# Bit search of a top-k threshold written out in three groups of blocks, with the mixer's operations placed singly among the bits

## The chip, the cores and the metric

The kernel runs on one core of a Trainium2 chip. The metric is the device time of one execution, in microseconds (us). The kernel is written with its own semaphores and its own order of instructions on every engine: TensorE (PE), VectorE (DVE), ScalarE (ACT), GpSimd (POOL) and SyncE (SP).

## The reference, cut to what matters

The whole is a two-layer decoder trunk over 1024 positions of width 1024. The change touches one stage of layer 0. There, every query position picks the 256 keys with the largest indexer scores, and mixer A, a short gated convolution, is computed beside it:

```python
isc = jnp.where(causal[None], isc, -jnp.inf)      # scores, Q_BLOCK = 128 queries at a time
_, idx = lax.top_k(isc, topk)                     # topk = 256
...
bg, cg, hv = jnp.split(sc, 3, axis=-1)            # 3 x 512 columns of h @ w_in
ya = bg * causal_dwconv(cg * hv, conv_w)          # CONV_WIDTH = 3
```

Only the threshold, the 256th largest score of each query, has to be found before the attention can mask its keys.

## The kernel before

**Blocks.** Queries are cut into 8 blocks of 128; block b has a score tile of 128 partitions (one query each) by 128(b+1) keys. Blocks 0 and 1 have at most 256 keys and need no search. The six others are searched together: DVE counts blocks 5, 4 and 3 (768, 640 and 512 columns), ACT counts blocks 7, 6 and 2 (1024, 896 and 384 columns).

**Search.** The threshold is built bit by bit, 31 times after the sign. Each round needs, for every block, the number of scores that reach a candidate. DVE's `count` is a `tensor_scalar` that compares and accumulates; ACT's is a `Sign` activation that accumulates. Then six candidates, one column each of the tile `srch` (128 partitions by 11 rows by 8), are updated together: `S_TRY` is the candidate with the next bit flipped (L1965, two tensors), the counts are compared with a row of limits (L1971, two tensors), the outcome is compared with the sign (L1972, two tensors), and L1974 (a `scalar_tensor_tensor`) shifts it into place and writes the new candidates. Both engines run a loop over bits. ACT counts all three of its blocks, and only then is `act_counted` raised; DVE writes all six candidates at once, and `cand_ready` lets both engines into the next bit.

**Mixer A.** PE computes 12 weight units (`ev_sc`, four tiles of three) of 48 matmuls each (`three_pass`, L859) into pairs of PSUM banks. POOL splits each unit's weights into a high and a low part beforehand: `w_scaled` (L592), `w_hi` (L593), `w_lo` (L595); the split of unit n+2 waits until PE has finished unit n. Tile i of the mixer is computed after bits 8i to 8i+7 (the last after seven bits) by `mixer_a(i)` on both engines, in one piece: ACT copies the first unit out (L1437), DVE multiplies it by the second (L2023), ACT makes the first tap (L1439), DVE adds the other two taps (L2028, twice) and multiplies by the third unit (L2033), ACT makes the high half (L1442) and DVE the low half (L2036). PE's next unit of a kind waits for the copy of the last one of that kind (`a_cg`, `a_prod`, `a_f`).

**After it.** PE waits for the last `a_f` and then computes the first attention scores (L1223); DVE masks them (L2066), in a stage written out by hand (`attend`), into which the end of the search (`resolve`) is placed. `ev_out`, the feed-forward layers and layer 1 follow.

The setup of the search is `search_begin`: it adds the causal mask to each tile, counts once against zero for the sign and writes the first candidates (L1946).

Of the kernel before, what the change touches and what calls it, by code (L numbers as in the profile page):

```python
# [27 lines left out]
P = 128  # L28
# [39 lines left out]
BY_DVE = [5, 4, 3]  # L68
BY_ACT = [7, 6, 2]
SEARCH = BY_DVE + BY_ACT  # L70
SIGN_BIT = -2 ** 31
# [16 lines left out]
def build(nc, t, out, stop=None):  # L88
    ctx = ExitStack()
    with ctx:  # L90
# [98 lines left out]
        (S_V, S_CAND, S_COUNT, S_NEG, S_TAKE, S_NEGI, S_BIT, S_NEAR, S_TRY, S_BACK, S_LIM) = range(11)  # L189
# [591 lines left out]
        def _(pe):  # L781
# [420 lines left out]
            with pe.Fori(0, 2) as i:  # L1202
                for ti in range(2):
                    tile = i * 2 + ti
                    for g in range(3):
                        unit = unit0["ev_sc"] + i * 6 + 3 * ti + g
                        pe.wait_ge((a_cg, a_prod, a_f)[g], tile + 1)
                        pe.wait_ge(w_split, unit + 1)
                        last = three_pass((3 * ti + g) % 2, 8, h_hi, h_lo, 0, pair((1, 2, 3 * ti)[g]), True, True)
                        last.then_inc(unit_done, 1)  # L1210


# [79 lines left out]
        def _(act):  # L1292
# [140 lines left out]
            def mixer_a(i):  # L1433
                act.wait_ge(unit_done, ring0["ev_sc"] + 3 * i + 1)
                if i >= 1:
                    act.wait_ge(a_prod, i + 1)
                A(work[:, 0, :], pair(1), ACT.Copy, scale=W_UNSCALE).then_inc(a_cg, 1)  # L1437
                act.wait_ge(a_prod, i + 2)
                A(work[:, 2, :], work[:, 1, :], ACT.Copy,  # L1439
                  scale=vec[:, VEC_AT["sc_conv"] + 8 + i:VEC_AT["sc_conv"] + 9 + i]).then_inc(a_tap, 1)  # L1440
                act.wait_ge(a_f, i + 3)
                A(mix_hi[:, i, :], work[:, 1, :], ACT.Copy).then_inc(a_hi, 1)  # L1442


            def count_bits(first, n):
                with act.Fori(0, n) as i:
                    act.wait_ge(cand_ready, i + (first + 1))
                    for j, b in enumerate(BY_ACT):
                        c = len(BY_DVE) + j
                        ins = A(signs[j], score[b][:], ACT.Sign, bias=srch[:, S_CAND, c:c + 1],  # L1450
                                accum_out=srch[:, S_COUNT, c:c + 1])
                    ins.then_inc(act_counted, 1)

            for i in range(4):
                count_bits(8 * i, 8 if i < 3 else 7)
                mixer_a(i)
# [241 lines left out]
        def _(dve):  # L1698
# [225 lines left out]
            next_bit, place = srch_i[:, S_BIT, 0:1], srch_i[:, S_BIT, 1:2]  # L1924
# [5 lines left out]

            def search_begin():
                for c, b in enumerate(SEARCH):
                    L = P * (b + 1)
                    V.memset(srch[:, S_LIM, c:c + 1], float(2 * TOPK - 1 - L) if b in BY_ACT else TOPK - 0.5)
                    ts_(V.tensor_tensor(score[b][:, L - P:L], score[b][:, L - P:L], causal_add[:], ALU.add))
                ts_(V.memset(srch[:, S_V, 0:NS], 0.0))
# [7 lines left out]
                V.memset(next_bit, 1 << 29)  # L1944
                ts_(V.memset(place, 31))
                V.tensor_scalar(srch_i[:, S_CAND, allc], srch_i[:, S_V, allc], 1 << 30, None, ALU.bitwise_or).then_inc(cand_ready, 1)  # L1946

            BIT_STEPS = 6

            def search_bits(first, n):  # L1950
                base = steps[0]
                with dve.Fori(0, n) as i:
                    at = [0]

                    def sb_(ins):
                        at[0] += 1
                        ins.then_inc(top_step, 1)
                        dve.wait_ge(top_step, i * BIT_STEPS + (base + at[0]))

                    dve.wait_ge(cand_ready, i + (first + 1))  # L1960
                    for c, b in enumerate(BY_DVE):
                        ins = count(S_CAND, b, c)
                    ins.then_inc(top_step, 1)
                    at[0] += 1
                    sb_(V.tensor_tensor(srch_i[:, S_TRY, allc], srch_i[:, S_CAND, allc], next_bit.broadcast_to([P, NS]),  # L1965
                                        ALU.bitwise_xor))
                    V.tensor_scalar(next_bit, next_bit, 1, None, ALU.logical_shift_right).then_inc(top_step, 1)
                    at[0] += 1
                    sb_(V.tensor_scalar(place, place, -1, None, ALU.add))
                    dve.wait_ge(act_counted, i + (first + 1))  # L1970
                    sb_(V.tensor_tensor(srch[:, S_TAKE, allc], srch[:, S_COUNT, allc], srch[:, S_LIM, allc], ALU.is_ge))  # L1971
                    sb_(V.tensor_tensor(srch_i[:, S_NEGI, allc], srch[:, S_TAKE, allc], srch[:, S_NEG, allc], ALU.is_equal))  # L1972
                    dve.sem_inc(dve_passed, 1)
# [112 lines left out]
            for i in range(4):  # L2086
                search_bits(8 * i, 8 if i < 3 else 7)
                mixer_a(i)
# [306 lines left out]
```

## Time and profile before

| what | value |
|---|---|
| time, median of 3 runs | 2456.72 us (2456.47 to 2457.64) |
| the profiled execution | 2457.84 us, span 2456.1 us |
| busy in the span | PE 2218.8, DVE 1343.9, POOL 1128.5, ACT 890.9 us |
| mean granted TensorE clock | 0.93 of full speed |
| window 193.0 to 359.9 us, all on the tile `srch` | DVE busy 126.89 us, ACT busy 88.83 us |

The span is the time from the first to the last instruction in the profile; the run's own time is 1.7 us longer. Busy time is summed by engine; a share over the whole span says little about this stage, in which the engines wait for each other in turn.

### The profile page before, as it was taken

What the parts mean: (1) busy time and instruction counts of PE and PEld (TensorE: products, weight loads), DVE (VectorE), ACT (ScalarE), POOL (GpSimd) and SP (SyncE); (2) the same over time, 40 slices, a digit from 0 to 9 for tenths busy, and PEclk for the clock granted to TensorE, in tenths of its full rate; (3) what the DMA queues carried; (4) which work ended last, traced back from release to release, by engine and by line L of the source; (5) the groups of instructions that cost most, each with busy time, mean ns of one, the idle gap of its engine ahead of it and who ended that gap; (6) DMA issues with size and microseconds to landing.
All of it is one profiled execution on the core that took longest, in us unless ns stands there. A gap on an engine that the chain in (4) does not pass through costs nothing. (4 is left out here: it accounts for less than half of the span.)

```text
span 2456.1 us, 30269 instructions
## 1 busy us (share of the span) xinstructions
PE 2218.8 (90%) x11622; PEld 1113.3 (45%) x11622; DVE 1343.9 (55%) x1816; ACT 890.9 (36%) x1193; POOL 1128.5 (46%) x749
## 2 busy tenths in 40 slices
PE   5777866789999999999997989889999999999998
PEld 3433324554434444444443444786443444444444
DVE  6778888853776146416641032983376614651662
ACT  5244565631554045215321212421145414531530
POOL 5102313304784667456448012321468566746642
PEclk7888887999999999999998999658999999999999
DMA  4000100002112111211123000000211212221112
GB/s 155 18 0 26 35 25 1 18 10 60 35 52 69 52 52 52 69 52 52 33 76 86 17 18 26 27 1 1 68 35 52 63 41 63 57 60 53 52 33 94
DMA packets 185977, 109.72 MB, mean 45 GB/s; under 512 B 3871, under 2 KB 180422, under 8 KB 185878
## 3 DMA queue, kind: packets, MB, share of 16 engines
q1 hardware_dynamic: 185414, 107.00, 15.1%
q0 software_dynamic: 464, 1.39, 0.2%
q8 instruction: 63, 1.03, 0.2%
q14 instruction: 36, 0.29, 0.0%
HBM read 104.18 MB, written 4.19 MB: 44 GB/s over the span
## 5 line engine op out<-in xcount | busy, mean ns | idle before, releaser
L592 POOL TENSOR_SCALAR w_scaled<-stage 128x1024 f32<-128x1024 f32 (+1 forms) x100 | 107.5, 1075 | 839.2 <-PE ps L859 642.1
L859 PE MATMUL ps<-arena,w_hi 128*128 128x512 f16 x1568 | 404.5, 381 | 7.6 <-POOL arena L772 2.8
L935 PE MATMUL ps<-h_hi,arena 128*128 128x512 f16 x1280 | 391.4, 381 | 11.6 <-DVE arena L2138 6.5
L935 PE MATMUL ps<-arena 128*128 128x512 f16 x1440 | 317.3, 379 | 0.2 <-POOL arena L667 0.2
L2094 DVE SCALAR_TENSOR_TENSOR xT<-ps,xT 128x1024 f32 (+1 forms) x64 | 78.4, 1225 | 410.9 <-PE ps L859 367.3
L935 PE MATMUL ps<-h_lo,arena 128*128 128x512 f16 x640 | 243.8, 381 | 0.0
L859 PEld LDWEIGHTS ps<-arena,w_hi 128*128 128x128 f16 x1568 | 153.6, 98 | 195.2 <-issue 9.1
L2147 DVE SCALAR_TENSOR_TENSOR work<-ps,fvec,work 128x1023 f32<-128x1023 f32 (+1 forms) x176 | 221.4, 1279 | 25.7 <-ACT work L1519 22.6
L859 PE MATMUL ps<-arena,w_lo 128*128 128x512 f16 x784 | 234.1, 380 | 0.0
L935 PEld LDWEIGHTS ps<-arena 128*128 128x128 f16 x1440 | 140.7, 98 | 170.6 <-POOL arena L667 1.2
L935 PEld LDWEIGHTS ps<-h_hi,arena 128*128 128x128 f16 x1280 | 125.7, 98 | 166.3 <-issue 14.5
L595 POOL TENSOR_TENSOR w_lo<-w_scaled,w_hi 128x1024 f16<-128x1024 f32 (+1 forms) x92 | 190.4, 2069 | 7.7
L1519 ACT ACTIVATE work<-ps,fvec 128x1024 f32<-128x1024 f32 x88 | 105.2, 1203 | 195.0 <-DVE ps L2138 195.0
L859 PE MATMUL ps<-h_hi,w_hi 128*128 128x512 f16 x352 | 108.9, 392 | 62.1 <-ACT work L1437 40.8
L1310 ACT ACTIVATE stage<-stage 128x2048 f32<-128x2048 f32 x36 | 68.8, 1910 | 215.2 <-DMA stage<-in_ffn_w_up_dram 215.2
L859 PEld LDWEIGHTS ps<-arena,w_lo 128*128 128x128 f16 x784 | 76.9, 98 | 93.1 <-issue 1.1
L2157 DVE TENSOR_TENSOR work<-work 128x1024 f32<-128x1024 f32 x44 | 103.7, 2357 | 28.0 <-ACT work L1524 28.0
L661 POOL TENSOR_TENSOR arena<-arena 128x1024 f16<-128x1024 f32 x40 | 116.8, 2920 | 0.0
L649 POOL TENSOR_TENSOR arena<-stage,arena 128x1024 f16<-128x1024 f32 x36 | 83.0, 2305 | 66.7 <-ACT arena L1329 66.7
L2138 DVE TENSOR_TENSOR ps<-stat,ps 128x512 f32<-128x512 f32 x80 | 55.7, 696 | 102.4 <-PE ps L935 98.2
L1450 ACT ACTIVATE stat<-arena,srch 128x1024 f16<-128x1024 f32 (+2 forms) x93 | 86.0, 926 | 62.9 <-DVE srch L1974 51.8
L859 PE MATMUL ps<-h_lo,w_hi 128*128 128x512 f16 x352 | 108.5, 391 | 0.0
(358 smaller groups left out, 3899.6 us busy)
## 6 DMA issues: line engine op xcount, KB each, us to landing
stage<-in_ffn_w_up_dram SPq DMA_DIRECT2D x76, 512.0 KB, 4.4
stage<-in_ffn_w_down_dram SPq DMA_DIRECT2D x32, 512.0 KB, 4.0
stage<-in_od_w_in_dram SPq DMA_DIRECT2D x20, 512.0 KB, 3.8
stage<-in_ev_w_in_dram SPq DMA_DIRECT2D x12, 512.0 KB, 3.8
arena<-in_ffn_w_up_dram SPq DMA_DIRECT2D x12, 512.0 KB, 4.8
stage<-in_ffn_w_down_dram SPq DMA_DIRECT2D x16, 384.0 KB, 3.4
arena<-in_x_dram SPq DMA_DIRECT2D x8, 512.0 KB, 6.9
stage<-in_ev_w_out_dram SPq DMA_DIRECT2D x8, 512.0 KB, 3.9
```

Source lines behind the costliest of these rows:

```text
L592: nc.gpsimd.tensor_scalar(scaled, src, W_SCALE, 1.0, ALU.mult, ALU.mult).then_inc(w_parts, 1)
L595: nc.gpsimd.tensor_tensor(lo, scaled, hi, ALU.subtract).then_inc(w_split, 1)
L649: G.tensor_tensor(lo[:, 0:1024], raw_of(layer, f, 0), hi[:, 0:1024], ALU.subtract)
L661: G.tensor_tensor(lo[:, 2560:3584], sums_b.rearrange("p s c -> p (s c)"), hi[:, 2560:3584], ALU.subtract).then_inc(su_split, 1)
L859: last = mm(out2[:, hf * HALF:(hf + 1) * HALF], w, a[:, k0 + k, hf * HALF:(hf + 1) * HALF], start=(first and k == 0 and pss == 0), stop=(l ...
L935: last = mm(ps[:, bank, :], left, right[:, k, :], start=(fresh and k == 0 and pss == 0), stop=(k == 3 and pss == 2), skip_group_check=True)
L1310: A(raw_pair(layer, f), raw_pair(layer, f), ACT.Copy, scale=W_SCALE).then_inc(su_scaled, 1)
L1450: ins = A(signs[j], score[b][:], ACT.Sign, bias=srch[:, S_CAND, c:c + 1], accum_out=srch[:, S_COUNT, c:c + 1])
L1519: A(work[:, 2 * fi + g, :], pair(2 * fi + g), ACT.Identity, bias=fvec[:, layer, f + (6 + g) * FT:f + (6 + g) * FT + 1], scale=fvec[:, laye ...
L2094: V.scalar_tensor_tensor(out=xT[:, m, :], in0=pair(pair0 + mi), scalar=W_UNSCALE, in1=xT[:, m, :], op0=ALU.mult, op1=ALU.add).then_inc(x_a ...
L2147: V.scalar_tensor_tensor(out=acc[:, s:], in0=y[:, 0:T - s], scalar=fvec[:, layer, tap:tap + 1], in1=acc[:, s:], op0=ALU.mult, op1=ALU.add) ...
L2157: V.tensor_tensor(work[:, 2 * fi + 1, :], work[:, 2 * fi, :], work[:, 2 * fi + 1, :], ALU.mult).then_inc(hid_f, 1)
```

## The change

1. The loops over bits are written out, 31 bits on each engine. Blocks are dealt anew: DVE counts blocks 4, 3 and 2 (640, 512, 384 columns), ACT counts 7, 6 and 5 (1024, 896, 768).
2. The six blocks form three groups: ACT's first block (7), ACT's others (6, 5), DVE's (4, 3, 2). Each group has its own rise of `act_counted` and `cand_ready`, so ACT may begin the next bit's block 7 as soon as that block's candidate is written.
3. The update of a candidate becomes two operations with one tensor input each: `take` (count against an immediate limit, times the bit) and `next_candidate` (xor with the old candidate and with a flip mask, both as one-column scalar operands, one instruction per block). `flip` makes the next mask for all six.
4. The operations of `mixer_a` are placed singly: in bits 8i+2 to 8i+7 (`mixer_gate`, `mixer_prod`, `mixer_tap`, `mixer_taps`, `mixer_high`, `mixer_low`). DVE's part comes after its counts of the bit.
5. PE's 12 units are written out; they use the four PSUM pairs in turn, so PE may be four units ahead of the mixer.
6. `search_begin` loses the row of limits, the counters `next_bit` and `place`, and the waits between the six mask additions; it gains two small operations for the flip masks.

```diff
-BY_DVE = [5, 4, 3]
-BY_ACT = [7, 6, 2]
+BY_DVE = [4, 3, 2]
+BY_ACT = [7, 6, 5]
+SEARCH_BITS = 31
+MIX_PROD, MIX_TAPS, MIX_LOW = 4, 6, 7
...
+            for n in range(12):
+                pe.wait_ge((a_cg, a_prod, a_f)[n % 3], 1)
+                if n >= 4:
+                    i0, g0 = divmod(n - 4, 3)
+                    pe.wait_ge((a_cg, a_prod, a_f)[g0], i0 + (2, 2, 3)[g0])
+                pe.wait_ge(w_split, unit0["ev_sc"] + n + 1)
+                three_pass(n % 2, 8, h_hi, h_lo, 0, pair(n % 4), True, True).then_inc(unit_done, 1)
...
+            first, *others = BY_ACT
+            for bit in range(SEARCH_BITS):
+                i, r = divmod(bit, 8)
+                act.wait_ge(cand_ready, 3 * bit - 1 if bit else 1)
+                sign_count(first).then_inc(act_counted, 1)
+                if r == MIX_TAPS + 1:
+                    mixer_high(i)
+                act.wait_ge(cand_ready, 3 * bit if bit else 1)
+                for b in others:
+                    last = sign_count(b)
+                last.then_inc(act_counted, 1)
+                if r == MIX_PROD - 2:
+                    mixer_gate(i)
+                if r == MIX_PROD:
+                    mixer_tap(i)
+                if r == MIX_TAPS and bit == SEARCH_BITS - 1:
+                    mixer_high(i)
...
+            def flip(bit):
+                out, three = srch_i[:, flips[bit % 2], allc], srch_i[:, S_TRY, allc]
+                shift = SEARCH_BITS - 2 - bit
+                op = ALU.logical_shift_left if shift >= 0 else ALU.logical_shift_right
+                flip_at[bit % 2] = step_(V.tensor_scalar(out, three, shift if shift >= 0 else -shift, None, op))
...
+            def take(bit, c0, c1, limit):
+                return V.tensor_scalar(srch_i[:, S_TAKE, c0:c1], srch[:, S_COUNT, c0:c1], float(limit),
+                                       2.0 ** (SEARCH_BITS - 1 - bit), ALU.is_ge, ALU.mult)
+            def next_candidate(bit, c):
+                cand = srch_i[:, S_CAND, c:c + 1]
+                return V.tensor_scalar(cand, srch_i[:, S_TAKE, c:c + 1], cand, srch_i[:, flips[bit % 2], c:c + 1],
+                                       ALU.bitwise_xor, ALU.bitwise_xor)
+            def search_bit(bit, between):
+                first, *others = BY_ACT
+                dve.wait_ge(act_counted, 2 * bit + 1)
+                took = step_(take(bit, ND, ND + 1, 2 * TOPK - 1 - P * (first + 1)))
+                dve.wait_ge(top_step, took)
+                next_candidate(bit, ND).then_inc(cand_ready, 1)
+                dve.wait_ge(cand_ready, 3 * bit + 1)
+                for c, b in enumerate(BY_DVE):
+                    last = count(S_CAND, b, c)
+                counted = step_(last)
+                if bit + 1 < SEARCH_BITS:
+                    flip(bit + 1)
+                between()
+                dve.wait_ge(act_counted, 2 * bit + 2)
+                for c, b in enumerate(others, ND + 1):
+                    last = take(bit, c, c + 1, 2 * TOPK - 1 - P * (b + 1))
+                others_took = step_(last)
+                dve.wait_ge(top_step, counted)
+                took = step_(take(bit, 0, ND, TOPK - 0.5))
+                dve.wait_ge(top_step, others_took)
+                for c in range(ND + 1, NS):
+                    last = next_candidate(bit, c)
+                last.then_inc(cand_ready, 1)
+                dve.wait_ge(top_step, took)
+                for c in range(ND):
+                    last = next_candidate(bit, c)
+                last.then_inc(cand_ready, 1)
...
+            def mixer_part(bit):
+                i, r = divmod(bit, 8)
+                if r == MIX_PROD:
+                    mixer_prod(i)
+                if r == MIX_TAPS:
+                    mixer_taps(i)
+                if r == MIX_LOW:
+                    mixer_low(i)
```

## Rows read from the trace of the kernel before

**Rows 1.** Waits, 184 to 385 us: who waited for whom; us in total, times, longest.

```profile
ACT stat L1450 <- DVE srch L1974: 51.8, 27, 3.7
PE ps L859 <- ACT work L1437: 40.8, 3, 16.3
```

**Rows 2.** Timeline of DVE, first bit: start us, us, engine, line.

```profile
193.20 1.01 DVE L1928 TENSOR_SCALAR_CACHE_REDUCE arena<-arena,srch 128x768 uint8<-128x768 f32 x1
...
196.17 0.73 DVE L1971 TENSOR_TENSOR srch<-srch 128x6 f32<-128x6 f32 x1
...
197.26 1.86 DVE L1974 SCALAR_TENSOR_TENSOR srch<-srch 128x6 int32<-128x6 int32 x1 [0.16 <-DVE srch L1972]
199.15 1.01 DVE L1928 TENSOR_SCALAR_CACHE_REDUCE arena<-arena,srch 128x768 uint8<-128x768 f32 x1
```

**Rows 3.** Timeline of DVE: the last operation that the search and the mixer hold back.

```profile
368.53 0.28 DVE L2066 CUSTOM_DVE_ANT_0 arena<-ps,arena 128x128 f32<-128x128 f32 x1
```

**Rows 4.** Timeline of POOL: the first split of a unit's weights, and the next.

```profile
194.84 1.05 POOL L592 TENSOR_SCALAR w_scaled<-stage 128x1024 f32<-128x1024 f32 x1 [124.69 <-PE ps L859]
...
196.97 2.12 POOL L595 TENSOR_TENSOR w_lo<-w_scaled,w_hi 128x1024 f16<-128x1024 f32 x1
205.20 1.05 POOL L592 TENSOR_SCALAR w_scaled<-stage 128x1024 f32<-128x1024 f32 x1 [6.10 <-PE ps L859]
```

**Rows 5.** The instructions of four lines: duration ns min/median/max, first and last start.

```profile
L1965 DVE TENSOR_TENSOR srch<-srch x31: 159/161/1782, 195.6 to 358.6; 128x6 int32<-128x6 int32 x31
...
L1971 DVE TENSOR_TENSOR srch<-srch x31: 166/167/1939, 196.2 to 359.1; 128x6 f32<-128x6 f32 x31
...
L1974 DVE SCALAR_TENSOR_TENSOR srch<-srch x31: 225/225/1860, 197.3 to 359.6; 128x6 int32<-128x6 int32 x31
...
L1969 DVE TENSOR_SCALAR srch<-srch x31: 142/144/145, 196.0 to 358.9; 128x1 int32<-128x1 int32 x31
```

**Rows 6.** Groups on DVE by form, 184 to 385 us: busy us, mean ns.

```profile
L1928 DVE TENSOR_SCALAR_CACHE_REDUCE arena<-arena,srch 128x768 uint8<-128x768 f32 x32 | 32.4, 1012 | 5.0 <-DVE srch L1974 4.7
L1928 DVE TENSOR_SCALAR_CACHE_REDUCE arena<-arena,srch 128x640 uint8<-128x640 f32 x32 | 28.0, 875 | 0.0
...
L1974 DVE SCALAR_TENSOR_TENSOR srch<-srch 128x6 int32<-128x6 int32 x31 | 18.4, 594 | 4.9 <-DVE srch L1972 4.9
L1971 DVE TENSOR_TENSOR srch<-srch 128x6 f32<-128x6 f32 x31 | 12.5, 405 | 1.9 <-ACT stat L1450 1.1
L1965 DVE TENSOR_TENSOR srch<-srch 128x6 int32<-128x6 int32 x31 | 9.5, 305 | 0.0
```

**Rows 7.** Timeline of DVE: the mixer's first tile, up to the next bit's first count.

```profile
231.74 1.23 DVE L2023 SCALAR_TENSOR_TENSOR work<-ps,work 128x1024 f32<-128x1024 f32 x1
234.19 2.60 DVE L2028 SCALAR_TENSOR_TENSOR work<-work,vec 128x1023 f32<-128x1023 f32 x2 [1.22 <-ACT work L1439]
...
239.17 1.23 DVE L2036 TENSOR_TENSOR arena<-work,arena 128x1024 f16<-128x1024 f32 x1 [1.12 <-ACT arena L1442]
240.31 1.01 DVE L1928 TENSOR_SCALAR_CACHE_REDUCE arena<-arena,srch 128x768 uint8<-128x768 f32 x1
```

**Rows 8.** Groups on ACT by form, 193 to 360 us.

```profile
L1450 ACT ACTIVATE stat<-arena,srch 128x1024 f16<-128x1024 f32 x31 | 35.6, 1148 | 62.9 <-DVE srch L1974 51.8 <-DVE srch L1946 11.1
L1450 ACT ACTIVATE stat<-arena,srch 128x896 f16<-128x896 f32 x31 | 31.9, 1028 | 0.0
...
L1437 ACT ACTIVATE work<-ps 128x1024 f32<-128x1024 f32 x4 | 4.0, 1003 | 0.0
L1439 ACT ACTIVATE work<-work,vec 128x1024 f32<-128x1024 f32 x3 | 3.4, 1149 | 4.3 <-DVE work L2023 4.3
```

**Rows 9.** Timeline of DVE, setup: a one-tensor operation alone, and beside POOL.

```profile
5.97 0.23 DVE L1726 TENSOR_SCALAR stat<-stat 128x128 f32<-128x128 f32 x1
...
6.62 0.32 DVE L1726 TENSOR_SCALAR stat<-stat 128x128 f32<-128x128 f32 x1
```

**Rows 10.** Timeline of POOL at the second of those.

```profile
6.53 0.32 POOL L576 TENSOR_TENSOR stat<-stat 128x64 f32<-128x64 f32 x1
```

More of the change, by code:

```diff
@@ L1436, in mixer_a, with mixer_tap @@
                     act.wait_ge(a_prod, i + 1)
-                A(work[:, 0, :], pair(1), ACT.Copy, scale=W_UNSCALE).then_inc(a_cg, 1)
+                A(work[:, 0, :], pair(3 * i % 4), ACT.Copy, scale=W_UNSCALE).then_inc(a_cg, 1)
+            def mixer_tap(i):
                 act.wait_ge(a_prod, i + 2)
@@ L1440, in mixer_a, with mixer_high, sign_count @@
                   scale=vec[:, VEC_AT["sc_conv"] + 8 + i:VEC_AT["sc_conv"] + 9 + i]).then_inc(a_tap, 1)
+            def mixer_high(i):
                 act.wait_ge(a_f, i + 3)
                 A(mix_hi[:, i, :], work[:, 1, :], ACT.Copy).then_inc(a_hi, 1)
[L1445 to L1456, printed above, removed]
+            def sign_count(b):
+                c = SEARCH.index(b)
+                return A(signs[c - len(BY_DVE)], score[b][:], ACT.Sign, bias=srch[:, S_CAND, c:c + 1],
+                         accum_out=srch[:, S_COUNT, c:c + 1])
+            first, *others = BY_ACT
[15 more added lines that the diff above has]
+                    mixer_high(i)
             def evict(b, h):
@@ L1943, in search_begin @@
                 ts_(V.tensor_scalar(srch_i[:, S_V, 0:NS], srch_i[:, S_NEGI, 0:NS], 31, None, ALU.logical_shift_left))
-                V.memset(next_bit, 1 << 29)
-                ts_(V.memset(place, 31))
                 V.tensor_scalar(srch_i[:, S_CAND, allc], srch_i[:, S_V, allc], 1 << 30, None, ALU.bitwise_or).then_inc(cand_ready, 1)
[L1948 to L1973, printed above, removed]
-                    V.scalar_tensor_tensor(out=srch_i[:, S_CAND, allc], in0=srch_i[:, S_NEGI, allc], scalar=place,
-                                           in1=srch_i[:, S_TRY, allc], op0=ALU.logical_shift_left,
-                                           op1=ALU.bitwise_xor).then_inc(cand_ready, 1)
-                assert at[0] == BIT_STEPS, at
-                steps[0] += n * BIT_STEPS
@@ new lines, in search_begin @@
+                ts_(V.tensor_scalar(srch_i[:, S_TRY, allc], srch[:, S_NEG, allc], -2.0, 3.0, ALU.mult, ALU.add))
+                flip(0)
+            def take(bit, c0, c1, limit):
[5 more added lines that the diff above has]
+                                       ALU.bitwise_xor, ALU.bitwise_xor)
@@ L2015, in rank, with mixer_prod @@
                 dve.wait_ge(ranked, b - 1)
-            def mixer_a(i):
-                tap = VEC_AT["sc_conv"]
+            def mixer_prod(i):
                 dve.wait_ge(unit_done, ring0["ev_sc"] + 3 * i + 2)
@@ L2022, in mixer_a, with mixer_taps @@
                     dve.wait_ge(a_mix, i)
-                V.scalar_tensor_tensor(out=work[:, 1, :], in0=pair(2), scalar=W_UNSCALE, in1=work[:, 0, :],
+                V.scalar_tensor_tensor(out=work[:, 1, :], in0=pair((3 * i + 1) % 4), scalar=W_UNSCALE, in1=work[:, 0, :],
                                        op0=ALU.mult, op1=ALU.mult).then_inc(a_prod, 1)
+            def mixer_taps(i):
+                tap = VEC_AT["sc_conv"]
                 dve.wait_ge(a_tap, i + 1)
@@ L2085, in _ @@
             search_begin()
-            for i in range(4):
-                search_bits(8 * i, 8 if i < 3 else 7)
-                mixer_a(i)
+            for bit in range(SEARCH_BITS):
+                search_bit(bit, lambda: mixer_part(bit))
+            mixer_part(SEARCH_BITS)
             attend()
```

32 lines of the change are left out of this document (14 added, 18 removed).

## The prediction

> **What bounds the kernel now.** I read the page first: PE is busy for 90% of the span, so a gain has to come from a stretch in which PE waits. The chain that ended last covers only the last quarter of the span and does not reach layer 0. So I went to the waits of 184 to 385 us, then to the timelines of DVE, ACT and POOL. ACT's counts waited 51.8 us in 27 waits for L1974, and PE waited 40.8 us for the mixer's first copy [rows 1]. So neither PE nor ACT sets the pace here: the round trip of each bit does, with DVE in it all the time. The stage runs from the first count at 193.20 [rows 2] to the first masked score at 368.53 [rows 3], 175.33 us. PE's 12 units need less: POOL's splits, one behind each unit, start at 194.84 and 205.20 [rows 4], a unit each 10.36 us, 124.3 us in all.
>
> In the first bit L1971 takes 0.73 and L1974 1.86 us and ends at 199.12 [rows 2], which is when POOL's `w_lo` ends, 196.97 + 2.12 = 199.09 [rows 4]. Medians are 0.167 and 0.225 [rows 5]. So small operations with two tensors wait for a running POOL operation. In sum: L1974 18.4 - 31 x 0.225 = 11.4, L1971 12.5 - 5.2 = 7.3, L1965 9.5 - 5.0 = 4.5 [rows 5, 6], together 23.2 us, for ten splits (units 2 to 11) of 196.97 + 2.12 - 194.84 = 4.25 us each. That bit took 5.95 us, 193.20 to 199.15 [rows 2].
>
> One tile of the mixer takes 231.74 to 240.31, 8.57 us [rows 7]; four times that is 34.3. What is left is bits: 175.33 - 34.3 - 23.2 = 117.8, or 3.80 us for each of 31.
>
> **Part by part: a bit without the mixer.** ACT: 1.148 for 1024 columns, 1.028 for 896 [rows 8]; by the same step 0.908 for 768. These are 3.08 us, and ACT can now run them back to back, since block 7's candidate is due while ACT counts the others. DVE: three counts took 193.20 to 195.60, when L1965 begins [rows 2, 5], 2.40 us for 1920 columns; 128 columns are worth 1.012 - 0.875 = 0.137 [rows 6], so 384 fewer leave 1.99. Around them stand eleven small operations (four of `take` kind, six `next_candidate`, one `flip`). A one-column operation lasts 0.144 [rows 5], and independent ones overlap as the count at 240.31 does with the subtraction that ends at 240.40 [rows 7], by 0.09. So an independent one costs about 0.07, and one that is waited for about 0.2 (an estimate between the 0.167 and 0.225 of [rows 5]). `take` and `next` for block 7 with the wait for ACT: 0.1 + 0.2 + 0.07. Then 1.99, `flip` and three `take` 0.28, the wait 0.1, five `next` 0.35: 3.09 us. ACT and DVE are level. A `next_candidate` has two pointer operands, which no row shows on so small a tile; L1974 has one and is 0.06 longer than L1971 [rows 5]. With 0.06 on each of six, DVE needs 3.45. I take 3.2 us a bit, range 3.08 to 3.45. 31 bits: 99.2 (95.5 to 107).
>
> **The mixer among the bits.** The operations are the same, and both engines are full, so they are hardly hidden. `mixer_gate` adds ACT's 1.00 [rows 8]. `mixer_prod` stands on DVE ahead of the others' `take`: 1.23 [rows 7], then ACT's tap, 1.15 [rows 8], delays block 7 of the next bit; with two handovers of 0.25 this is 2.9. `mixer_taps` is 2.60 + 1.23 = 3.8 on DVE [rows 7], L2033 taken like L2023, in which ACT runs out of candidates. `mixer_high` and `mixer_low` (1.23 [rows 7]) overlap partly with the other engine's counts: 1.3. Sum 9.0, four times 36: a little more than the 34.3 of before. What is queued behind a mixer operation is always a `take`, and behind that both engines. New costs: taps and lows now run beside splits. They have two SBUF tensors, a split covers 4.25 of each 10.36 us, and half of 1.05 or 2.12 us is what such a wait costs: 3 operations x 0.41 x 0.8 = 1.0 for each of three tiles, 3.0. Mixer in all 39. PE is no wait in it: unit 2 is done at about 194.8 + 2 x 10.36 = 215.5 [rows 4], and `mixer_taps` of the first tile is reached at about 193 + 6 x 3.2 + 1.0 + 2.9 + 2.3 = 218.
>
> **POOL beside the new small operations.** Two per bit have several columns: `flip` (6) and DVE's own `take` (3). One-column operations never waited: 142 to 145 ns in 31 cases [rows 5], though the loop had ten splits beside it. A one-tensor operation on 128 columns did: 0.23 alone, 0.32 beside POOL's operation from 6.53 to 6.85, ending at 6.94 [rows 9, 10]. In between there is no row. Bounds: nothing, if three and six columns go as one does; 23.2 us, if they wait as three two-tensor operations a bit did. As they are two and stand together, with one wait in most hit bits, half: 12 us. I take the 12, since the operation with several columns is the same kind as in [rows 9], and ends with POOL's as the two-tensor ones do.
>
> The Trainium skill, SBUF — State Buffer, section "Who interferes with whom", has the rule: two-input operations contend with GpSimd's reads, and a `tensor_scalar` without accumulator output may enter a two-port mode and contend as well. By it `flip` and `take` of three columns wait and the accumulating counts do not; the trace agrees for 128 columns (0.32 beside 0.23), and no row shows three or six. With it the sum comes to 2431, without it to 2419, as below.
>
> **Setup and PE.** Six mask additions without waits, and no limits to set: 0.6 us less. PE's 12 units now end about 194.8 + 11 x 10.36 = 309 [rows 4], some 30 us before the search: writing them out is worth nothing by itself, it keeps PE out of the chain. Of `ev_sc` nothing is later, and SP's loads follow the splits as before. Behind the search everything waits for DVE, so the gain arrives whole at the end.
>
> **Sum.** 99.2 + 39 + 12 = 150.2 against 175.3, and 0.6: 25.7 us less. The profiled execution would go from 2457.84 (span 2456.1 and 1.7 around it) to 2432.1; it stood 1.1 above the median of the runs, so they go from 2456.7 to 2431.
>
> **Rivals.**
> 1. *The several-column operations don't wait for POOL.* For it: the one-column rows [rows 5]. Against: [rows 9]. Then 12 us fewer, 2419; with ACT's floor of 3.08 a bit 2415.
> 2. *The small operations don't overlap* (slower). `take`, `flip` and `next` run strictly after each other at 0.23 (L1974 [rows 5]): 11 x 0.23 + 1.99 + 0.1 = 4.6 a bit, 143 in all; with 39 and 12, and 0.6 off, this is 18 us more, 2474, and without the 12 it is 2462. It decides from (175.3 + 0.6 - 51)/31 = 4.03 a bit on. Against it: the three counts' durations, 1.012 + 0.875 + 0.738 = 2.63 [rows 6], took 2.40, so each overlaps by 0.08, and so does the pair at 240.31 [rows 7].
> 3. *The gain doesn't arrive*: PE, now idle for some 30 us ahead of the attention, or the attention's own rounds give back half of it or all: 2444 to 2457. Against: what follows is released by DVE's L2066 [rows 3], and nothing in the change touches it.
>
> **How the numbers follow.** Forecast 0.50, own range 2423 to 2443 (3.08 to 3.45 a bit: 4 less or 8 more; POOL's share 8 to 16: 4 either way). Rival 1 0.34, rival 2 0.06, rival 3 0.10. The range 2413 to 2446 takes the forecast, rival 1 down to its floor and 2 below it, and POOL's upper bound of 23.2 (2442). 0.2% is 4.9 us and about what the measurement tells from no change. Faster: forecast, rival 1 and half of rival 3, 0.89; same 0.05; slower 0.06.
>
> **What would show it.** Plain bits of 3.1 to 3.4 us on ACT with hardly a wait; L1974's 51.8 us of ACT waits down to some 15, in the mixer's bits; the longest `flip` and `take` of three columns near 1 to 2 us where a split runs and one-column ones at 0.15; PE's last unit at 309; the first L2066 at about 343 instead of 368.53 [rows 3]. Wrong if the small operations start more than 0.15 apart, if ACT waits in plain bits, or if the attention that follows is longer than before.

## The result, and the profile after

The changed kernel takes 2433.15 us, median of 4 runs (2432.04 to 2439.64), against 2456.81 for the kernel before on the same chip: a ratio of 0.9907, 95% interval 0.9894 to 0.9921. The forecast was 2431 in a range of 2413 to 2446. Its profiled execution took 2433.86 us with a span of 2432.1, 24.0 less than before. The runs of one kernel vary by up to 10 us, and their mean granted clock varies with them (last section), so where a kernel ran once or a few times the length of the stage in the trace decides and not the time.

The waits of 184 to 360 us, which answer to [rows 1]:

```profile
PE ps L1221 <- DVE work L2069: 34.6, 1, 34.6
ACT stat L1448 <- DVE srch L1980: 17.5, 16, 2.8
ACT arena L1444 <- DVE work L2069: 15.3, 4, 4.6
...
DVE srch L1974 <- ACT stat L1448: 5.8, 5, 1.2
```

ACT's counts waited 51.8 us for the bit's last operation and wait 17.5 now, some of it in plain bits (a bit without a part of the mixer), as in this one (timeline of ACT):

```profile
200.99 1.04 ACT L1448 ACTIVATE stat<-arena,srch 128x896 f16<-128x896 f32 x1 [0.42 <-DVE srch L1980]
```

PE stood still three times among the mixer's tiles and now has all its units done and waits once, for the last product.

A plain bit on DVE, and one beside a split, where [rows 2] had 5.95 us (timeline of DVE; columns start us, us, engine, line):

```profile
198.18 0.87 DVE L1939 TENSOR_SCALAR_CACHE_REDUCE arena<-arena,srch 128x640 uint8<-128x640 f32 x1
...
200.18 0.17 DVE L1953 TENSOR_SCALAR srch<-srch 128x6 int32<-128x6 int32 x1
200.25 0.28 DVE L1974 TENSOR_SCALAR srch<-srch 128x1 int32<-128x1 f32 x3
200.50 1.00 DVE L1980 TENSOR_SCALAR srch<-srch 128x1 int32<-128x1 int32 x5
201.41 0.15 DVE L1974 TENSOR_SCALAR srch<-srch 128x1 int32<-128x1 f32 x1
201.59 0.27 DVE L1980 TENSOR_SCALAR srch<-srch 128x1 int32<-128x1 int32 x1
201.78 0.87 DVE L1939 TENSOR_SCALAR_CACHE_REDUCE arena<-arena,srch 128x640 uint8<-128x640 f32 x1
...
207.48 1.85 DVE L1953 TENSOR_SCALAR srch<-srch 128x6 int32<-128x6 int32 x1
```

The bit takes 201.78 - 198.18 = 3.60 us and has no idle time. Its counts take 2.00, `flip` and the three `take` to 200.50 0.32, the five `next_candidate` (L1980) 0.91, and block 7's `take` and `next_candidate` 0.37. The last row is a `flip` that lasts 1.85 instead of 0.17 us. It ends at 209.33, and POOL's `w_lo` at 209.31 (timeline of POOL, as [rows 4]):

```profile
207.17 2.14 POOL L597 TENSOR_TENSOR w_lo<-w_scaled,w_hi 128x1024 f16<-128x1024 f32 x1
```

DVE's groups of 180 to 362 us by form, against [rows 5, 6] (busy us, mean ns, idle time before):

```profile
L1980 DVE TENSOR_SCALAR srch<-srch 128x1 int32<-128x1 int32 x186 | 39.4, 267 | 1.1
...
L1953 DVE TENSOR_SCALAR srch<-srch 128x6 int32<-128x6 int32 x31 | 12.5, 402 | 0.0
L1974 DVE TENSOR_SCALAR srch<-srch 128x1 int32<-128x1 f32 x93 | 10.9, 144 | 5.8 <-ACT stat L1448 5.8
...
L1974 DVE TENSOR_SCALAR srch<-srch 128x3 int32<-128x3 f32 x31 | 8.1, 260 | 0.0
```

`flip` alone lasts 0.17, 31 times that is 5.2, so its waits are 7.3 us. The three-column `take` at 0.144 gives 4.5 and 3.6 of waits: 10.9 us beside POOL, predicted as 12. By the lengths of the bits it is 10.3: by so much the ten bits with such a wait are longer than the same bits without one. Neither of the one-column groups shows any.

The mixer's first tile, where [rows 7] had it in one piece: the product, the last `take` of that bit, and the first tap.

```profile
212.83 1.22 DVE L2056 SCALAR_TENSOR_TENSOR work<-ps,work 128x1024 f32<-128x1024 f32 x1
...
216.40 0.15 DVE L1974 TENSOR_SCALAR srch<-srch 128x1 int32<-128x1 f32 x1 [1.19 <-ACT stat L1448]
...
223.20 1.28 DVE L2064 SCALAR_TENSOR_TENSOR work<-work,vec 128x1023 f32<-128x1023 f32 x1
```

The end of the stage, which answers to [rows 3]:

```profile
343.98 1.23 DVE L2074 TENSOR_TENSOR arena<-work,arena 128x1024 f16<-128x1024 f32 x1
345.12 0.28 DVE L2113 CUSTOM_DVE_ANT_0 arena<-ps,arena 128x128 f32<-128x128 f32 x1
```

And ACT's counts (groups by form, against [rows 8]), 3.09 us a bit in all:

```profile
L1448 ACT ACTIVATE stat<-arena,srch 128x1024 f16<-128x1024 f32 x31 | 35.1, 1133 | 10.2 <-DVE srch L1968 10.2
L1448 ACT ACTIVATE stat<-arena,srch 128x896 f16<-128x896 f32 x31 | 32.1, 1036 | 18.0 <-DVE srch L1980 17.5
L1448 ACT ACTIVATE stat<-arena,srch 128x768 f16<-128x768 f32 x31 | 28.5, 919 | 0.0
```

The stage, from DVE's first count of a bit (193.93) to the first masked score (345.12), takes 151.19 us; before it took 175.33. That is 24.1 less. It begins 0.7 later (193.93 against 193.20), and what follows it takes 2432.1 - 345.12 = 2087.0 instead of 2456.1 - 368.53 = 2087.6, 0.6 less. 24.1 - 0.7 + 0.6 = 24.0: the whole difference of the spans, made in this stage. That the rest agrees to 0.6 us is in part chance: in twelve of the fourteen traces here it lasts between 2084.9 and 2089.1 us, in the other two 2093.4 and 2094.4.

### The profile page after: what moved, and what is told of

It reads as the page before. It is cut to its first block and busy times, and to the rows that moved or that the text cites. A ratio compares the mean times of both kernels' runs of the same rounds, so it can differ in the third digit from the quotient of the medians.

```text
span 2432.1 us, 30028 instructions
## 1 busy us (share of the span) xinstructions
PE 2212.7 (91%) x11622; PEld 1111.0 (46%) x11622; DVE 1335.3 (55%) x1964; ACT 899.6 (37%) x1193; POOL 1129.0 (46%) x749
## 5 line engine op out<-in xcount | busy, mean ns | idle before, releaser
L2194 DVE SCALAR_TENSOR_TENSOR work<-ps,fvec,work 128x1023 f32<-128x1023 f32 (+1 forms) x176 | 221.4, 1279 | 25.6 <-ACT work L1530 22.5
L861 PE MATMUL ps<-h_hi,w_lo 128*128 128x512 f16 x352 | 106.1, 383 | 0.0
```

The costliest lines, as they stand in the source:

```text
L861: last = mm(out2[:, hf * HALF:(hf + 1) * HALF], w, a[:, k0 + k, hf * HALF:(hf + 1) * HALF], start=(first and k == 0 and pss == 0), stop=(l ...
L2194: V.scalar_tensor_tensor(out=acc[:, s:], in0=y[:, 0:T - s], scalar=fvec[:, layer, tap:tap + 1], in1=acc[:, s:], op0=ALU.mult, op1=ALU.add) ...
```

## The experiments

"Stage" is always this length, first count of a bit to first masked score, in the profiled execution. Times are medians, with a ratio to the kernel before where there were several rounds. Small edits are against the changed kernel, the one of e8 against the kernel before. They are shortened: `S_TAKE[c]` stands for column c of that row of `srch`.

| | stage | plain bit | waits for POOL | time (runs) |
|---|---|---|---|---|
| before | 175.33 | 3.78 | 23.2 | 2456.8 |
| after | 151.19 | 3.60 | 10.9 | 2433.2 (4) |
| e1 no pointers | 136.45 | 3.07 | 7.5 + 2.6 | 2418.3 (1) |
| e2 one pointer | 143.51 | 3.24 | 10.4 + 2.6 | 2434.1 (1) |
| e3 one column | 150.84 | 3.94 | 0 + 0.2 | 2433.4 (4) |
| e4 tap later | 147.49 | 3.60 | 12.4 | 2433.3 (4) |
| e5 old deal | 157.95 | 4.00 | 5.7 | 2440.6 (1) |
| e6 mixer whole | 158.76 | 3.60 | 12.4 + 1.9 | 2448.5 (1) |
| e7 one group | 171.12 | 4.83 | 8.8 + 0.7 | 2450.4 (1) |
| e8 before, unrolled | 174.01 | 3.64 | 27 | 2457.0 (10) |
| e9 flip table | 141.21 | 3.58 | 0 + 1.0 | 2423.5 (1) |
| e10 table and tap | 138.65 | 3.58 | 0 + 3.3 | 2421.1 (4) |
| e11 two tensors | 152.07 | 3.07 | some 24 + 1.3 | 2433.1 (1) |
| e12 low by POOL | 132.17 | 3.58 | 0 + 1.4 | 2422.7 (4) |

Ahead of the plus sign are the waits of the small operations, as busy time beyond the duration alone (0.167 for `flip`, 0.144 for `take`), summed as above; behind it those of the mixer's taps and low halves, where any waited.

### The price of a pointer: e1, e2

```diff
 # e1: both pointers become constants
-    V.tensor_scalar(cand, S_TAKE[c], cand, flips[bit % 2][c], bitwise_xor, bitwise_xor)
+    V.tensor_scalar(cand, S_TAKE[c], 1 << 29, 1 << 28, bitwise_xor, bitwise_xor)
 # e2: one of them
+    V.tensor_scalar(cand, S_TAKE[c], flips[bit % 2][c], 1 << 29, bitwise_xor, bitwise_xor)
```

> The two pointer operands of next_candidate are replaced by immediates, so the candidates are no longer the reference's; every instruction, wait and tile stays. In the changed kernel these operations start 0.18 us apart. Theory A (the pointer operands cost it): they now start about 0.07 apart, DVE needs 3.60 - 6 x 0.11 = 2.94 us a bit, and the plain bit falls to ACT's floor of 3.07 to 3.15. The search shrinks by some 13 to 15 us, to about 2419. Rival B (it is the price of a small integer xor, whatever its operands): they stay 0.18 apart and the time stays at 2433.

> next_candidate keeps the flip mask as its one pointer operand; the other is an immediate, so the candidates are not the reference's. Theory A: one pointer costs half of two, 0.12 to 0.13 us from start to start, a plain bit of about 3.27 and a time of about 2423. Theory A': the price is for having a pointer at all, and the operations stay 0.18 apart, bit 3.60, 2433. Rival B: 0.18 as well; only together with the run without pointers can it be told from A'.

Measured: 136.45 and 143.51 us, 14.7 and 7.7 less than after. In e1 the same stretch of a bit reads (timeline of DVE):

```profile
198.66 0.40 DVE L1980 TENSOR_SCALAR srch<-srch 128x1 int32<-128x1 int32 x5
199.26 0.15 DVE L1974 TENSOR_SCALAR srch<-srch 128x1 int32<-128x1 f32 x1 [0.20 <-ACT stat L1448]
199.45 0.15 DVE L1980 TENSOR_SCALAR srch<-srch 128x1 int32<-128x1 int32 x1
```

and the groups, e1's and then e2's:

```profile
L1980 DVE TENSOR_SCALAR srch<-srch 128x1 int32<-128x1 int32 x186 | 17.1, 147 | 1.1
```

```profile
L1980 DVE TENSOR_SCALAR srch<-srch 128x1 int32<-128x1 int32 x186 | 28.2, 206 | 1.1
```

The mean goes 147, 206, 267 ns with no, one and two pointers: 60 ns each. Both kernels compute other candidates than the reference; every instruction and wait stays. It is not only latency: five operations that don't wait for each other take 0.40 us in e1 and 1.00 in the changed kernel, so their starts stand (0.40 - 0.15) / 4 = 0.06 and (1.00 - 0.27) / 4 = 0.18 apart. Six times 0.12 is 0.72 us a bit. The bit gets 0.53 shorter in e1, since DVE then waits 0.20 for ACT: it is at ACT's own 3.07, the floor that rival 1 of the prediction put at 3.08. e2's bit of 3.24 was expected at 3.27. In both, one pair of the mixer's taps now met a split, which took back 2.6 us. e2's time of 2434.1 would mislead: its stage is 7.7 us shorter, and what follows 7.4 us longer, at a lower granted clock.

### The several-column operations beside POOL: e3, e9

e3 writes the two that wait in single columns: seven instructions more a bit.

```diff
-    V.tensor_scalar(S_FLIP[0:6], S_TRY[0:6], shift, None, op)
+    for c in range(6): V.tensor_scalar(S_FLIP[c], S_TRY[c], shift, None, op)
-    took = step_(take(bit, 0, ND, TOPK - 0.5))
+    for c in range(ND): last = take(bit, c, c + 1, TOPK - 0.5)
+    took = step_(last)
```

> flip and DVE's own take are each written as one-column operations (6 and 3 instead of 1 and 1). Theory (operations of three and six columns wait for POOL's split, one-column ones never): none of flip and take lasts longer than 0.17 us any more, the 10.8 us of such waits go, and seven more operations 0.07 us apart add 0.49 us to each of 31 bits, 15.2 us. Plain bit 4.09 us, time 2433 - 10.8 + 15.2 = 2437.5. Rival (any small operation waits for POOL when it comes first, its columns do not matter): the one-column ones now show waits of 1 to 2 us, and the time is 2448.

Groups of e3 on DVE by form:

```profile
L1976 DVE TENSOR_SCALAR srch<-srch 128x1 int32<-128x1 f32 x186 | 16.4, 143 | 5.3 <-ACT stat L1448 5.3
L1953 DVE TENSOR_SCALAR srch<-srch 128x1 int32<-128x1 int32 x186 | 14.0, 144 | 0.0
```

372 one-column operations beside ten splits, with a mean of 143 and 144 ns and none above 154: none waited. The plain bit rose from 3.60 to 3.94 or 3.95 (4.09 was expected, at 0.07 for each of seven), 0.345 for seven operations, 0.05 each. 31 x 0.345 = 10.7 paid for some 10.5 won, so the stage stayed (150.84) and so did the time (2433.41, ratio 0.9899, 0.9883 to 0.9916). The equal time hides two effects of more than 10 us.

e9 takes the waits away without the price. All 31 shifted masks are made once, ahead of the search (POOL makes the row of shifts at the start), and the bits read them as pointers; `take` is in single columns.

```diff
+    V.tensor_scalar(flip_rows[30], S_TRY, 1, None, logical_shift_right)
+    V.tensor_tensor(flip_rows[0:30], S_TRY broadcast, shifts, logical_shift_left)
-    flip(bit + 1)                      # in each bit
-    ... flips[bit % 2][c] ...
+    ... flip_rows[bit][c] ...
```

> The flip masks of all 31 bits are made once, in search_begin, as a table; flip leaves the bits, and DVE's own take is written as three one-column operations. Theory (what is left of POOL's price is the 10.8 us of flip and take of several columns, and one-column operations cost 0.05 us each): a plain bit is 3.60 - 0.07 + 0.10 = 3.63 us, none waits for POOL, and the stage of 151.2 us falls to about 141.3. Rival (the waits only move to the next operation): no less than 148.

Stage 141.21 (expected 141.3), 2423.5 us. Its bits, from first count to first count, in us, eight to a line (the last up to the first masked score):

```
3.58 3.58 3.70 3.59 5.94 3.58 7.35 5.04
3.58 3.59 3.70 3.59 5.94 3.58 8.01 4.71
3.59 3.58 3.71 3.58 5.95 3.58 7.36 4.71
3.59 3.58 3.71 3.57 5.95 3.58 8.11
```

Outside the mixer every bit now has the same length, splits or not. The third of each eight holds the gate, the fifth the product, the seventh the taps, the eighth the low half. The stage lost 10.0 us: the 10.3 by which the splits had made bits longer and 0.6 of shorter bits, less about 1.0 that one pair of taps and one low half now wait for splits (8.01 beside 7.36, 5.04 beside 4.71).

### The mixer among the bits: e4, e6

In the changed kernel ACT's tap stands behind all three counts of its bit and delays block 7's count of the next: DVE waits 1.19 for it (the row at 216.40 above). e4 puts the tap behind that first count:

```diff
     sign_count(first).then_inc(act_counted, 1)
+    if r == MIX_PROD + 1: mixer_tap(i)
     ...
     last.then_inc(act_counted, 1)
-    if r == MIX_PROD: mixer_tap(i)
```

> ACT's mixer_tap is moved behind block 7's count of the next bit. In the changed kernel ACT stands idle for 2.06 us in bit 8i+4 until DVE's mixer_prod is done, then makes the tap, and only then counts block 7 of the next bit, for which DVE waits 1.2 us. Theory (this order is a wait of its own, not work): bit 8i+4 falls from 6.02 to 4.8 us in all four tiles, DVE's idle time of 5.8 us before take goes, 4.8 us less, 2428.5. Rival (ACT is full, so the tap only moves its 1.15 us to the next bit): 2433 to 2434.

Timeline of DVE in e4, the same bit:

```profile
212.90 1.22 DVE L2056 SCALAR_TENSOR_TENSOR work<-ps,work 128x1024 f32<-128x1024 f32 x1
214.03 0.28 DVE L1974 TENSOR_SCALAR srch<-srch 128x1 int32<-128x1 f32 x3
214.27 1.00 DVE L1980 TENSOR_SCALAR srch<-srch 128x1 int32<-128x1 int32 x5
215.18 0.15 DVE L1974 TENSOR_SCALAR srch<-srch 128x1 int32<-128x1 f32 x1
```

No wait for ACT is left; the bit falls from 6.02 to 4.73, 5.2 us over four tiles. The stage falls by 3.7 (147.49), since the waits for POOL rise by 1.5: bits that come earlier fall on other splits. The median of the time (2433.3; 2428.5 was expected) does not show it and would by itself speak for the rival: two runs at 2430.4 and 2431.0, two at 2435.6 and 2435.8. The trace excludes the rival: the tap's 1.15 us does not turn up in the next bit, which in the third and fourth tile takes a plain 3.60. This verdict rests on the trace alone.

e6 goes back to the mixer in one piece, after bits 7, 15, 23 and 30:

```diff
-    search_bit(bit, lambda: mixer_part(bit))
+    search_bit(bit, lambda: None)
+    if bit % 8 == 7 or bit == 30: mixer_prod(i); mixer_taps(i); mixer_low(i)
```

> The changed search, but each tile of the mixer in one piece after bits 7, 15, 23 and 30, as before the change. Theory (placing the operations singly saves little, since DVE is full and only ACT's share hides): one piece costs 8.6 us as it did before, against 7.4 now, so the stage of 151.2 us grows by 4 to 5 us. Rival A (singly placed operations are what the gain comes from): 10 us or more. Rival B (nothing): 0 to 1 us.

Stage 158.76, 7.6 more than after, where 4 to 5 were expected (in the time of 2448.5 the part after the stage has another 6.4 us more, as in e2). A bit with a whole tile took 12.16, 8.56 above a plain one, against 7.4 in single operations. The first took 14.06 (timeline of DVE, then of POOL, in e6):

```profile
226.65 1.22 DVE L2052 SCALAR_TENSOR_TENSOR work<-ps,work 128x1024 f32<-128x1024 f32 x1
229.09 4.49 DVE L2060 SCALAR_TENSOR_TENSOR work<-work,vec 128x1023 f32<-128x1023 f32 x2 [1.22 <-ACT work L1439]
```

```profile
229.06 2.12 POOL L597 TENSOR_TENSOR w_lo<-w_scaled,w_hi 128x1024 f16<-128x1024 f32 x1
```

Here is the wait of the taps for a split that the prediction charged with 3.0 us: 4.49 instead of 2.60, once, where the mixer's place in the bits let them meet. So about 4.5 of the 7.6 us (four times 8.56 - 7.43) is what the placing costs, and the rest is waits for POOL that fell otherwise: 1.9 here and 1.5 more in the small operations.

### The groups, the deal and the loop: e5, e7, e8

```diff
 # e5: the old deal of blocks
-BY_DVE = [4, 3, 2]; BY_ACT = [7, 6, 5]
+BY_DVE = [5, 4, 3]; BY_ACT = [7, 6, 2]
 # e7: one group; every candidate of a bit released together, all counts waited for together
-    dve.wait_ge(act_counted, 2 * bit + 1) ... take, next_candidate of block 7 ... then_inc(cand_ready, 1)
-    dve.wait_ge(act_counted, 2 * bit + 2)
+    dve.wait_ge(act_counted, bit + 1)
+    for c in (*range(ND, NS), *range(ND)): last = next_candidate(bit, c)
+    last.then_inc(cand_ready, 1)       # ACT likewise: one wait, one rise
 # e8: the kernel before, with its two loops written out and no semaphore for the loop
-    with dve.Fori(0, n) as i:
+    for i in range(n):
```

> The changed kernel with the blocks dealt as before: DVE counts 5, 4, 3 and ACT 7, 6, 2. Theory (DVE sets the plain bit, 3.60 us, ACT's 3.07 is covered): DVE has 384 columns more, 0.41 us a bit, so a plain bit takes 4.01 us and the stage from DVE's first count to the first masked score grows by some 12 us, from 151.2 to 163. Rival (ACT's counts set it): ACT has 384 columns fewer, and the bit gets shorter or stays.

> The changed kernel with the three groups joined again: one rise of act_counted and one of cand_ready a bit; the one-tensor operations, the deal and the mixer stay. Theory: the small operations of DVE no longer run beside ACT's counts. A plain bit is ACT's 3.07, 0.1 for the wait, four take at 0.05 to 0.07, six next_candidate at 0.18 and a last 0.1: 4.6 us against 3.60, the stage 31 us longer, about 182, which is above the 175.3 of before. Rival: ACT's counts of 3.07 and DVE's 2.0 were overlapped before as well, so the groups bring less than 15 us.

> The kernel before, with nothing changed but the loops over bits written out on ACT and DVE (and the semaphore step that its register waits needed). Theory: what the loop costs is the idle 0.41 us behind L1974 in most bits and the 0.16 us ahead of it, so a plain bit goes from 3.80 to about 3.4 us and the stage from 175.3 to about 163: half of the change's gain comes from here. POOL's 23 us stay. Rival (the turn of the loop was hidden behind ACT's start): 0 to 3 us.

e7: 171.12 us with all else of the change in place. So without the groups 19.9 of the 24.1 us are gone. Its bits show what they remove (timeline of DVE in e7):

```profile
198.98 0.17 DVE L1952 TENSOR_SCALAR srch<-srch 128x6 int32<-128x6 int32 x1
200.20 0.35 DVE L1973 TENSOR_SCALAR srch<-srch 128x1 int32<-128x1 f32 x4 [1.05 <-ACT stat L1448]
200.59 1.18 DVE L1979 TENSOR_SCALAR srch<-srch 128x1 int32<-128x1 int32 x6
201.80 0.88 DVE L1938 TENSOR_SCALAR_CACHE_REDUCE arena<-arena,srch 128x640 uint8<-128x640 f32 x1
```

DVE stands for 1.05 us until ACT has counted, then ACT stands while DVE combines: 4.83 us a bit, longer than the 3.78 of before, because from ACT's end to the next count there are now ten small operations (1.60 us) where there were three. Against 3.60, thirty-one bits make 38 us of that, and the stage is only 19.9 longer: with 149.7 in bits and 8.8 in waits, 12.6 are left for the mixer, which hides in the idle time there. The expectation of 182 had left that out.

e5: 157.95, 6.8 more than after (expected 163). The bit went to 4.00, by 0.40 for 384 more columns of counting on DVE, but the waits for POOL fell from 10.9 to 5.7. e8: 174.01, and not 163; the rival's 0 to 3 us is the size that came. The turn of the loop, with its semaphore step, which I took for 0.4 us a bit, is worth 3.78 - 3.64 = 0.14, or 4.3 in all, and the waits for POOL took back most of it: they rose from 23.2 to 27. The time is on average that of the kernel before (ratio 1.0003, 0.9991 to 1.0015), from five runs about 4 us below it and five about as much above. Writing the loops out is worth 1.3 us of stage by itself.

### What the pointers cost if they are avoided: e11

```diff
+    def xor2(row, c0, c1, a, b): V.tensor_tensor(srch[row, c0:c1], srch[a, c0:c1], srch[b, c0:c1], bitwise_xor)
+    xor2(S_NEGI, ..., S_CAND, this)    # ahead of the counts
-    next_candidate(bit, c)             # one per column, two pointers
+    xor2(S_CAND, ..., S_TAKE, S_NEGI)  # one per group
```

> The changed kernel with next_candidate made by two-tensor operations again, one for each group (six a bit in all: three that flip a bit of the candidate ahead of time and three that join the outcome), without pointer operands. Theory: beside no split, the six pointer operations of 0.18 us give way to six of 0.07 and a plain bit falls to ACT's 3.1 to 3.2; but now eight operations a bit can wait for POOL instead of two, which costs 25 us or more against 10.8: the stage is 148 to 155, no gain. Rival (the waits are bounded by the splits, not by the number of operations): the stage falls to about 140.

Many bits away from the splits reach 3.07, ACT's floor, as e1's do. The stage stays at 152.07 (148 to 155 expected) and the time at 2433.1 (groups of e11 on DVE by form):

```profile
L1984 DVE TENSOR_TENSOR srch<-srch 128x1 int32<-128x1 int32 x62 | 25.6, 413 | 1.7
L1974 DVE TENSOR_SCALAR srch<-srch 128x3 int32<-128x3 f32 x31 | 12.7, 409 | 0.0
L1984 DVE TENSOR_TENSOR srch<-srch 128x3 int32<-128x3 int32 x62 | 11.3, 183 | 0.0
```

One column with two tensors lasts 0.16 alone, and 62 of them took 25.6: 15.7 us of waits in these alone, with 8.2 in the `take` and 0.5 in `flip`. Even a single column waits for POOL if it has two tensors. What the pointers cost, about 15 us, goes to POOL instead.

### Put together: e10, e12

e10 is e9 with e4's tap. e12 also moves the mixer's low halves to POOL, behind its splits of units 5, 8 and 11:

```diff
+    for i in {5: (0,), 8: (1,), 11: (2, 3)}.get(u, ()):
+        pool.wait_ge(a_hi, i + 1)
+        gpsimd.tensor_tensor(mix_lo[i], work[1], mix_hi[i], subtract).then_inc(a_mix, 1)
-    if r == MIX_LOW: mixer_low(i)      # DVE
```

> The table and, as well, ACT's tap behind block 7's count of the next bit. The two act on different waits, so they should add: bit 8i+4 goes from 6.02 to 4.75, 1.27 us for four tiles, stage 136.3, and the time 15 us under the changed kernel: 2418. Rival (DVE's order leaves ACT late elsewhere): the stage stays above 139.

> Table, later tap, and the mixer's low halves (L2074, 1.2 us each on DVE) made by POOL between its splits. DVE is the full engine and POOL is idle for 6 of each 10.4 us: bit 8i+7 falls from 4.7 to about 3.6 and the last 1.2 us go, 4.6 in all, stage about 131.7, time about 2413. Rival (POOL's subtraction holds DVE back, or a split comes late for PE): stage 134 or more.

e10: stage 138.65, 2421.14 us, ratio 0.9858 (0.9839 to 0.9877). It was expected at 136.3 and 2418; in the third tile the taps, 2.60 us alone, now met a split (timeline of DVE in e10), less so in the first (3.30), and the first low half did too (2.07 for 1.22):

```profile
289.63 4.34 DVE L2064 SCALAR_TENSOR_TENSOR work<-work,vec 128x1023 f32<-128x1023 f32 x2
```

e12: stage 132.17 (expected 131.7), and the bit with the low half costs a plain 3.58 instead of 4.72. Some 1.1 of the 6.5 us that it gains on e10 only changed sides: the last low half stood ahead of the first masked score and now comes behind it, on POOL. And its time is 2422.7 (2413 expected), ratio 0.9858 (0.9841 to 0.9874), no better than e10's. What follows the first masked score takes 2417.6 - 332.32 = 2085.3 us in e10 and 2415.8 - 326.75 = 2089.1 in e12. A part of it is seen at the stage's end (timelines of DVE and POOL in e12):

```profile
327.17 1.78 DVE L2023 TENSOR_SCALAR srch<-srch 128x6 int32<-128x6 int32 x1
```

```profile
326.79 2.13 POOL L719 TENSOR_TENSOR arena<-work,arena 128x1024 f16<-128x1024 f32 x1 [30.91 <-ACT arena L1450]
```

The first operation behind the search has six columns and waits 1.6 us for POOL's last low half. The other 2.2 us belong to the attention as well: the first sum behind it (into the tile `xT`) starts 171.47 us after the first masked score in e10 and 175.16 in e12, which is 3.7 of the 3.8. In the first 50 us TensorE's granted clock was 0.76 in e10 and 0.69 in e12, in the next 50 it was 0.93 and 0.90. How much of the 2.2 us the clock makes, no run shows; it stays open (after the same mark the changed kernel has 2087.0). e10 and e12 both beat the changed kernel, by some 0.5%.

## Why the prediction held, step by step

The sum was right to one us (150.2 for 151.2 measured), and two of its three terms were not. Measured, they are 111.6 for the bits, 29.7 for the mixer and, by the lengths of the bits, 10.3 for POOL; less 0.4 for block 7's pair, which the last bit lacks, this is the stage, 151.2.

**A bit without the mixer: mis-sized.** Predicted 3.2 (own range 3.08 to 3.45), measured 3.60, so 111.6 and not 99.2. Three pieces were right: the counts (1.99, measured 2.00), `flip` with the `take` (0.28, measured 0.32), block 7's pair (0.37). The step that failed is "five `next` 0.35". It set a `next_candidate` at the 0.07 of any independent one-column operation. Measured, five take 0.91 us. The text did name the pointer as a cost and read 0.06 for it from L1974 against L1971 [rows 5], which e1 and e2 confirm to the digit. But it charged that once for an operation with two pointers, and then went below the 3.45 that this gave, with 3.2. The measured 3.60 is outside its own range. Two on each of six give 0.72: from e1's bit without its wait, 3.07 - 0.20 + 0.72 = 3.59. So DVE and ACT are not level; DVE is the bound by 0.5 us, and ACT waits for it in plain bits (the 0.42 us above), which the prediction had named as a mark of being wrong: it had put what was left of ACT's waits into the mixer's bits.

**The mixer: too dear.** Predicted 9.0 for each tile and 39 in all, measured 7.4 and 29.7. The bits with a part of it, less 3.60 and less POOL's waits: the gate 0.11 (predicted 1.00), product with tap 2.42 (2.9), taps 3.77 (3.8), high and low 1.13 (1.3). The gate is nearly free for the reason that made the bits too long: ACT counts for 3.09 of 3.60 us and has half a us to spare in each bit, and it is two bits ahead of the product. The runs bear this out: where ACT is the bound, in e1 (plain bit 3.07), the bit with the gate takes 3.98, in e2 3.89 for 3.24, and in e3 (3.94) no more than a plain one. "Both engines are full, so they are hardly hidden" followed from the wrong 3.2. The 3.0 for waits of taps and low halves never came: two-tensor operations on 1024 columns would wait, as e6's 4.49 us shows, but in the changed kernel none met a split. Where they fall is a matter of phase against PE's 10.36 us; in e10 two pairs of taps and a low half do.

**POOL beside the small operations: right.** Predicted 12, measured 10.9 by durations and 10.3 by the lengths of the bits; e9, which takes it away, gains 10.0 net. The reading from 128 columns [rows 9, 10] down to six and three held, and so did that from one column [rows 5]. The Trainium skill has the condition in VectorE: DVE Perf Modes, section "Mode 2×_2P — use both read ports for one tensor": a one-tensor operation uses the second port only where its outermost dimension that is not one is even, or odd and equal on both sides. A single column has none. By that rule six and three columns contend and one does not, and the trace agrees: 1.85 us for `flip` beside `w_lo`, 143 ns in 372 single columns of e3. Rival 1 (no waits, 2419) is excluded.

**Rival 2**, small operations that don't overlap: excluded for those without pointers (0.06 apart in e1 and e3), and half true for those with two, whose 0.18 is beyond the 0.15 that I had named as the mark of a wrong prediction. It did not decide, since the bit stayed under the 4.03 at which the change breaks even.

**Rival 3**, the gain given back: excluded. What follows the stage took 2087.0 us after 2087.6, and the medians differ by 23.7 us.

**Setup and the marks.** The first candidate is out 0.91 us earlier (192.07 for 192.98), but DVE's first count now waits for ACT's count of block 7 and comes 0.73 later; I had 0.6 in the other direction. PE's last unit ended soon after 308 (309 predicted), the first masked score came at 345.12 for 343, and ACT's waits fell to 17.5 for 15, though not where they were expected.

**Where the gain is from.** Undone alone: the groups 19.9 us (e7), the mixer singly 7.6 (e6), the deal 6.8 (e5). They add up to more than 24.1, since each covers a part of another: without groups, the mixer is hidden in idle time. The one-tensor `next_candidate`, replaced by two-tensor operations with all else kept, is worth 0.9 (e11). PE's part of the change, the four PSUM pairs, was not undone; no run prices it.

The two errors have opposite signs, 12.4 us in the bits and -9.3 in the mixer. Of the 9.3, the gate's 3.6 have the same root as the 12.4; 3.0 are waits that the phase happened to spare, and the other 2.7 are handovers and overlaps that cost less than was put on them. That the time came out within 2 us is mostly luck.

## What to carry to other kernels

Count pointer operands and not only instructions: on tiles of a few columns a per-partition pointer cost as much as another instruction (0.06 us), the two on each candidate here 15 us of a stage of 151. When two engines alternate on a loop of a few us, release the longest part first and let each count while the other combines; then price the slack of both, because an operation put on the one with slack is free (the gate) and on the other is not. And where an operation waits for another engine's port, ask for its phase: what was saved upstream moved other operations onto the splits, which gave back 1.5 of 5.2 us in e4 and most of the gain in e8.

## What the runs showed of the chip that was not expected

- A one-column operation on DVE starts 0.06 us after the one ahead of it if it doesn't wait for it, 0.12 with one pointer and 0.18 with two (e1, e2, after).
- One-tensor operations wait for POOL's with six and with three columns (up to 1.85 and about 2 us) and never with one (372 in e3, the longest 154 ns); two-tensor ones also with one (mean 413 ns for 160, e11).
- The turn of the loop, with its semaphore step, cost 0.14 us a bit (e8), a third of what I had put on it.
- Ten runs of e8 stand in two groups, five at 2452.9 to 2453.5 with a mean granted clock of 0.932 and five at 2460.4 to 2462.8 with 0.929. The runs of after and e4 differ in a similar way. No longer run of a kernel was traced beside a shorter one, but two traces, e2's and e6's, have some 7 us more behind the first masked score than the others. The windows of the changed kernel and of e2, 1200 to 1400 us after that mark, show where (columns: window, us, busy us of PE, weight loads, DVE, ACT, POOL, granted clock, DMA share, GB/s):

```profile
1545.10:1645.10 100.00, 88.75 (x754) 85.24 (x753) 79.24 (x79) 28.96 (x28) 25.52 (x12) 0.53 0.00 1
1645.10:1745.10 100.00, 97.14 (x464) 54.20 (x463) 38.60 (x28) 14.35 (x16) 28.45 (x20) 0.92 0.13 37
```

```profile
1538.00:1638.00 100.00, 88.74 (x727) 85.29 (x726) 77.43 (x76) 26.39 (x25) 25.53 (x12) 0.50 0.00 1
1638.00:1738.00 100.00, 99.62 (x457) 59.00 (x457) 37.71 (x28) 14.94 (x17) 25.18 (x17) 0.85 0.12 34
```

Ahead of the first window TensorE was busy for 90% at 0.90 in both. In that window e2 is at the lower of its two levels (1.2 of 2.4 GHz) throughout, and the changed kernel for nearly all of it; it also regains the upper one sooner, and shows 754 and 464 matmuls where e2 shows 727 and 457. In the same two windows e6 has 0.50 and 0.86, and all twelve others have 0.53 and 0.91 to 0.93. Some 900 to 1000 us after the mark it is the other way round: e2 and e6 had 0.91, the twelve others 0.86. What decides which of the two a run takes, none of the runs shows; e2's and e6's times are read with these 7 us in mind.
